# Local heads by pairs, and a new order for two engines around them

## The reference

```python
def window_attention(q, k, v, sink):
    ...
    s = jnp.einsum('bnqhgd,bnkhd->bnhgqk', qb, kb).astype(jnp.float32) / math.sqrt(HEAD_DIM)
    ...
    valid = (jnp.abs(dist) <= WINDOW) & (k_pos[:, None, :] >= 0) & (k_pos[:, None, :] < S)
    s = jnp.where(valid[None, :, None, None], s, NEG_INF)
    ...
    p = jax.nn.softmax(jnp.concatenate([s, sink_b], axis=-1), axis=-1)[..., :-1]
    o = jnp.einsum('bnhgqk,bnkhd->bnqhgd', p.astype(v.dtype), vb)
    return o.reshape(B, S, A_Q_HEADS * HEAD_DIM)
```

## Time and profile before

| | |
|---|---|
| median of 3 runs | 1089.72 us (1089.44 to 1089.85) |
| profiled execution | 1089.0 us, span 1087.1 us |
| PE busy | 1069.8 us, 98% of the span |
| PEld busy | 865.4 us, 80% |
| DVE busy | 726.7 us, 67% |
| ACT busy | 539.7 us, 50% |
| the chain of work that ended last | PE 89%, DVE 7%, ACT 2% |
| granted TensorE clock | full but for the first microseconds (mean 0.995) |

### The profile page before, as it was taken

One profiled execution on the slowest core, in us unless ns is written; L12 is line 12 of the kernel. 1 busy time (PEld: TensorE's weight loads), 2 busy tenths in 40 slices (PEclk: granted clock), 3 DMA queues, 4 the chain that ended last, 5 costly groups with the idle time before them and its releaser, 6 DMA issues.

```text
span 1087.1 us, 14671 instructions
## 1 busy us (share of the span) xinstructions
PE 1069.8 (98%) x4952; PEld 865.4 (80%) x4952; DVE 726.7 (67%) x1224; ACT 539.7 (50%) x829; POOL 37.1 (3%) x40
## 2 busy tenths in 40 slices
PE   8899999999999999999999999999999999999998
PEld 7677678888888778788888888887777888888886
DVE  5756875455557997754555578988868877454553
ACT  6454554444445546644444465547457546444452
POOL 3112000000000210000000000000000000000000
PEclk9899999999999999999999999999999999999999
DMA  9454255565665544455655553544444365655653
GB/s 287 120 167 148 79 167 182 192 190 178 191 193 172 163 152 133 153 180 192 190 178 191 194 172 114 160 155 136 136 138 152 129 199 177 191 182 188 192 184 107
DMA packets 133599, 182.18 MB, mean 168 GB/s; under 512 B 11446, under 2 KB 80322, under 8 KB 133490
## 3 DMA queue, kind: packets, MB, share of 16 engines
q1 hardware_dynamic: 132090, 178.32, 51.7%
q0 software_dynamic: 1056, 2.70, 1.2%
q10 hardware_dynamic: 408, 0.56, 0.1%
HBM read 180.49 MB, written 1.05 MB: 167 GB/s over the span
## 4 chain that ended last, share of the span: by engine, by line
PE 89%; DVE 7%; ACT 2%; issue 1%; DMA 1%; POOL 0%; SPq 0%; DVEq 0%; POOLq 0%; ACTq 0%
PE ps L1844 17%; PE ps L1855 16%; PE ps L1847 16%; PE ps L1865 7%; PE ps L1866 7%; PE ps L1870 7%; PE ps L1829 2%; PE ps L1831 2%; PE ps L1830 2%; DVE wlo L1013 2%; PE ps L1939 1%; PE ps L1922 1%; ACT whi L538 1%; PE ps L2402 1%; PE ps L2069 1%
## 5 line engine op out<-in xcount | busy, mean ns | idle before, releaser
L1013 DVE TENSOR_TENSOR wlo<-raw,whi 128x1024 fp32r<-128x1024 f32 (+1 forms) x338 | 403.7, 1225 | 106.3 <-ACT whi L538 105.3
L538 ACT ACTIVATE whi<-raw 128x1024 fp32r<-128x1024 f32 (+1 forms) x338 | 342.2, 1053 | 102.6 <-DMA raw<-in_ffn_w_out 28.2
L1844 PE MATMUL ps<-whi,ath 128*128 128x512 f32 (+1 forms) x896 | 357.9, 400 | 3.1 <-ACT whi L538 1.4
L1847 PE MATMUL ps<-whi,atl 128*128 128x512 f32 (+1 forms) x896 | 349.7, 391 | 0.0
L1855 PE MATMUL ps<-wlo,ath 128*128 128x512 f32 (+1 forms) x896 | 240.6, 390 | 0.0
L1844 PEld LDWEIGHTS ps<-whi,ath 128*128 128x128 f32 x896 | 168.9, 189 | 47.1 <-issue 8.3
L1855 PEld LDWEIGHTS ps<-wlo,ath 128*128 128x128 f32 x896 | 167.7, 188 | 35.4 <-DVE wlo L1013 0.5
L1847 PEld LDWEIGHTS ps<-whi,atl 128*128 128x128 f32 x896 | 169.1, 189 | 33.0 <-issue 0.5
L1865 PE MATMUL ps<-whi,brh 128*128 128x512 f32 x272 | 106.5, 392 | 0.4 <-issue 0.4
L1866 PE MATMUL ps<-whi,brl 128*128 128x512 f32 x272 | 105.9, 389 | 0.0
L1089 DVE TENSOR_TENSOR brl<-ps,brh 128x512 fp32r<-128x512 f32 x33 | 22.8, 692 | 93.7 <-ACT brh L584 93.7
(11 more groups left out here) (344 smaller groups left out, 1009.1 us busy)
## 6 DMA issues: line engine op xcount, KB each, us to landing
raw<-in_ffn_w_in SPq DMA_DIRECT2D x176, 256.0 KB, 2.9
raw<-in_ffn_w SPq DMA_DIRECT2D x132, 256.0 KB, 2.9
raw<-in_w_in SPq DMA_DIRECT2D x104, 256.0 KB, 2.9
raw<-in_ffn_w_out SPq DMA_DIRECT2D x88, 256.0 KB, 2.8
raw<-in_a_w_in SPq DMA_DIRECT2D x48, 256.0 KB, 4.1
raw<-in_b_w_in SPq DMA_DIRECT2D x48, 256.0 KB, 3.0
raw<-in_a_w_out SPq DMA_DIRECT2D x16, 256.0 KB, 2.9
raw<-in_b_w_out SPq DMA_DIRECT2D x16, 256.0 KB, 2.8
```

Source lines behind the costliest of these rows:

```text
L538: a_(unit_view(whi, slot, w), unit_view(raw, slot, w), ACT.Copy).then_inc(hi_ready, 1)
L1013: v_.tensor_tensor(unit_view(wlo, slot, w), unit_view(raw, slot, w), unit_view(whi, slot, w), ALU.subtract).then_inc(lo_ready, 1)
L1844: mm(ps[bk + t][:, 0:w], ath[:, k, t * P:(t + 1) * P], rh[:, kk, :], start=k == 0, stop=False)
L1847: mm(ps[bk + t][:, 0:w], atl[:, k, t * P:(t + 1) * P], rh[:, kk, :], start=False, stop=False)
```

## The change

Scores and products with the values are issued for two heads at once. `w_scores(i)` takes heads 2i and 2i + 1, alternating between partitions 0 to 63 and 64 to 127 with each matmul; `w_pv(i)` does the same with the two halves of the output. The semaphores count accordingly. `C_L` and the small columns beside it are used in four copies in place of two, so that logits may run up to four heads ahead. `C_PT` still has two, so ACT's copy of a head's transposes now waits for the product pair before. PE's list becomes: between any two pieces of two units one head's transposes; with those of the even heads the score pair for two heads ahead and the product pair before; for the last head the pieces are of one unit. DVE's and ACT's lists are written anew: DVE does the three Newton steps in one go and puts the split of unit `U_C + 47` behind the last `w_out`. No instruction of the three engines is added or left out, but for the semaphores' waits.

```diff
             def w_exp(h):
-                c = sm[:, 128 + 16 * (h % 2):]
+                c = sm[:, 128 + 16 * (h % 4):]
...
             def w_pt(h):
                 act.wait_ge(sem("w_p_turned"), h + 1)
+                if h >= 2:
+                    act.wait_ge(sem("w_pv"), h // 2)
                 a_(C_PT[:, h % 2, :], ps[6 + h % 2][:, :], ACT.Copy).then_inc(sem("w_pt"), 1)
 
             def w_out(i):
-                act.wait_ge(sem("w_pv"), 2 * i + 2)
+                act.wait_ge(sem("w_pv"), i + 1)
                 a_(brh[:, i, :], ps[2 + i % 2][:, 0:S], ACT.Copy).then_inc(sem("w_out_hi"), 1)
...
-            for i in range(WQ + 2):
-                if i == 1:
-                    evac(19, lambda t: C_pd[:, t, 1024:1536], n=4, tiles=(0, 1))
-                if i == 3:
-                    gate_evac(20, 0)
-                if i == 5:
-                    gate_evac(21, 1)
-                if i == 7:
-                    gate_evac(22, 0)
+            w_exp(0)
+            feed(W_STEPS[0])
+            evac(19, lambda t: C_pd[:, t, 1024:1536], n=4, tiles=(0, 1))
+            w_exp(1)
+            w_pt(0)
+            act.wait_ge(sem("h_z"), 4)
+            a_(obh[:, :, :], h_v, ACT.Copy).then_inc(sem("h_hi"), 1)
+            for i in range(WQ // 2):
+
+                feed(W_STEPS[2 * i + 1])
+                if i < 3:
+                    w_exp(2 * i + 2)
                 if i == 0:
-                    w_exp(0)
-                if i < WQ:
-                    feed(W_STEPS[i])
-                if 0 < i < WQ:
-                    w_exp(i)
-                if i == 0:
-                    act.wait_ge(sem("h_z"), 4)
-                    a_(obh[:, :, :], h_v, ACT.Copy).then_inc(sem("h_hi"), 1)
-                if 0 <= i - 1 < WQ:
-                    w_pt(i - 1)
-                if i == WQ:
-                    feed(W_STEPS[WQ])
-                if i == 1:
                     act.wait_ge(evac_act, ACT_EVACS[18])
                     c_squares([(C_z, C_pd[:, 0, 0:1024]), (hid_flat, C_pd[:, 1, 0:512]),
                                (sil_flat, C_pd[:, 1, 512:1024])])
-                if i >= 3 and i % 2 == 1:
-                    w_out((i - 3) // 2)
+                w_pt(2 * i + 1)
+                if i < 3:
+                    feed(W_STEPS[2 * i + 2])
+                    w_exp(2 * i + 3)
+                    gate_evac(20 + i, (0, 1, 0)[i])
+                    w_out(i)
+                    w_pt(2 * i + 2)
+            feed(W_STEPS[WQ])
+            w_out(3)
...
             def w_logits(h):
                 dve.wait_ge(sem("w_scores"), h + 1)
-                if h >= 2:
-                    dve.wait_ge(sem("w_p_turned"), h - 1)
-                c = sm[:, 128 + 16 * (h % 2):]
+                if h >= 4:
+                    dve.wait_ge(sem("w_p_turned"), h - 3)
...
-            for i in range(WQ + 2):
-                if 1 <= i - 1 < WQ:
-                    w_prob(i - 1)
-                if i < WQ:
-                    w_logits(i)
-                if i == 0:
-                    feed(U_C + 32)
-                    w_prob(0)
-
-                if i == 5:
-                    d_sines(0)
-                if i == 6:
-                    d_cosines(0)
-                if i == 7:
-                    d_add(0)
-                    d_sines(1)
-                if i == 8:
-                    d_cosines(1)
-                    d_add(1)
-                    d_scale_keys()
-                if i < WQ:
-                    feed(W_STEPS[i])
-                if i >= 3 and i % 2 == 1:
-                    w_out((i - 3) // 2)
-
-                if i == 1:
-                    dve.wait_ge(sem("h_hi"), 1)
-                    v_.tensor_tensor(obl[:, :, :], h_v, obh[:, :, :], ALU.subtract).then_inc(sem("h_lo"), 1)
-                if i == 2:
-                    c_sums(3, C_z, 320, 16)
-                if i == 3:
-                    c_sums(4, hid_flat, 336, 8)
-                    c_sums(5, sil_flat, 344, 8)
-                if i == 4:
-                    dve.wait_ge(sem("c_ssq"), 6)
-                    link(v_.tensor_scalar(rq_a[:, 0:32], sm[:, 320:352], 1.0 / HD, EPS, ALU.mult, ALU.add))
-                    rsqrt_guess(sm[:, 320:352], 32)
-                if 4 <= i < 7:
-                    rsqrt_step(sm[:, 320:352], 32)
-                if i == 6:
-                    q_scale = sm[:, 320:352].rearrange("p (t h) -> p t h", t=NT)[:, :, 0:8]
-                    link(v_.tensor_scalar(q_scale, q_scale, float(HD) ** -0.5, None, ALU.mult))
+            w_logits(0)
+            feed(U_C + 32)
+            w_prob(0)
+            w_logits(1)
+            feed(W_STEPS[0])
+            w_prob(1)
+            w_logits(2)
+            feed(W_STEPS[1])
+            w_logits(3)
+            dve.wait_ge(sem("h_hi"), 1)
+            v_.tensor_tensor(obl[:, :, :], h_v, obh[:, :, :], ALU.subtract).then_inc(sem("h_lo"), 1)
+            w_prob(2)
+            feed(W_STEPS[2])
+            c_sums(3, C_z, 320, 16)
+            w_prob(3)
+            w_logits(4)
+            feed(W_STEPS[3])
+            w_out(0)
+            w_logits(5)
+            c_sums(4, hid_flat, 336, 8)
+            c_sums(5, sil_flat, 344, 8)
+            w_prob(4)
+            feed(W_STEPS[4])
+            dve.wait_ge(sem("c_ssq"), 6)
+            link(v_.tensor_scalar(rq_a[:, 0:32], sm[:, 320:352], 1.0 / HD, EPS, ALU.mult, ALU.add))
+            rsqrt(sm[:, 320:352], 32)
+            w_prob(5)
+            w_logits(6)
+            feed(W_STEPS[5])
+            w_out(1)
+            w_logits(7)
+            d_sines(0)
+            w_prob(6)
+            feed(W_STEPS[6])
+            q_scale = sm[:, 320:352].rearrange("p (t h) -> p t h", t=NT)[:, :, 0:8]
+            link(v_.tensor_scalar(q_scale, q_scale, float(HD) ** -0.5, None, ALU.mult))
+            w_prob(7)
+            d_cosines(0)
+            d_add(0)
+            feed(W_STEPS[7] - 1)
+            w_out(2)
+            d_sines(1)
+            d_cosines(1)
+            d_add(1)
+            d_scale_keys()
+            w_out(3)
+            feed(W_STEPS[7])
             feed(U_OA + 4)
...
-            def w_scores(h):
-                if h == 0:
+            def w_scores(i):
+
+                if i == 0:
                     pe.wait_ge(sem("c_w_copied"), 3)
-                if h >= 2:
-                    pe.wait_ge(sem("w_l"), 2 * (h - 1))
-                g, pr = h // 4, h // 2
-                rows = slice(64 * (h % 2), 64 * (h % 2) + 64)
+                else:
+                    pe.wait_ge(sem("w_l"), 4 * i)
                 for t in range(NT):
-                    ins = mm(ps[4 + h % 2][:, t * S:(t + 1) * S], C_qT[rows, pr, t * P:(t + 1) * P], C_kT[rows, g, :],
-                             start=True, stop=True)
-                ins.then_inc(sem("w_scores"), 1)
+                    for f in range(2):
+                        rows = slice(64 * f, 64 * f + 64)
+                        ins = mm(ps[4 + f][:, t * S:(t + 1) * S], C_qT[rows, i, t * P:(t + 1) * P],
+                                 C_kT[rows, i // 2, :], start=True, stop=True)
+                ins.then_inc(sem("w_scores"), 2)
...
-            def w_pv(h):
-                pe.wait_ge(sem("w_pt"), h + 1)
-                i = h // 2
-                if h % 2 == 0 and i >= 2:
+            def w_pv(i):
+
+                pe.wait_ge(sem("w_pt"), 2 * i + 2)
+                if i >= 2:
                     pe.wait_ge(sem("w_out_lo"), i - 1)
-                if h == 0:
+                if i == 0:
                     pe.wait_ge(evac_act, ACT_EVACS[18])
-                rows = slice(64 * (h % 2), 64 * (h % 2) + 64)
-                g = h // 4
+                g = i // 2
                 for s in range(2):
-                    ins = mm(ps[2 + i % 2][rows, 0:S], C_pa[:, s, 640 + g * HD:640 + (g + 1) * HD],
-                             C_PT[:, h % 2, s * S:(s + 1) * S], start=(s == 0), stop=(s == 1))
+                    for f in range(2):
+                        rows = slice(64 * f, 64 * f + 64)
+                        ins = mm(ps[2 + i % 2][rows, 0:S], C_pa[:, s, 640 + g * HD:640 + (g + 1) * HD],
+                                 C_PT[:, f, s * S:(s + 1) * S], start=(s == 0), stop=(s == 1))
                 ins.then_inc(sem("w_pv"), 1)
 
+            def w_turn(h):
+                p_turn(h, "w_p", "w_pt", "w_p_turned", C_L[:, h % 4, :])
+
             w_scores(0)
+            units(19, 2, 4)
+            w_turn(0)
             w_scores(1)
-            w_pieces = [(19, 2, 4), (20, 0, 2), (20, 2, 4), (21, 0, 2), (21, 2, 4), (22, 0, 2), (22, 2, 4), (23, 0, 2)]
-            for h in range(WQ + 1):
-                if h < WQ:
-                    units(*w_pieces[h])
-                    p_turn(h, "w_p", "w_pt", "w_p_turned", C_L[:, h % 2, :])
-                if h + 2 < WQ:
-                    w_scores(h + 2)
-                if h >= 1:
-                    w_pv(h - 1)
+            units(20, 0, 2)
+            w_turn(1)
```

(29 more changed lines are left out.)

## The result

The changed kernel took 1078.42 us (median of 4 executions, 1074.50 to 1081.68), the kernel before 1089.58 (4 executions, 1087.35 to 1089.85; three of them are those that the prediction started from): ratio 0.9908, interval 0.988 to 0.9936. The profiled execution, however, took 1081.68 us with a span of 1079.8, and 1079.8 is the span that the prediction gave.

The account below looks back on a forecast made before the run. PE was taken to bound the local heads' 67.17 us; its interludes were to fall from 19.64 to 12.37 us, so 7.3 off the median 1089.72 gave 1082.4 us, range 1081.5 to 1086.3.

Parts of the forecast that it names:

- What bounds the stretch: Eight local heads, 67.17 us: PE sets the length, so PE time spared is won until DVE, idle 8.05, becomes later.
- Score pair 1.07, product pair 1.03: PE, local heads: two heads' scores take 1.07 us and two heads' products 1.03, the array halves running side by side.
- The new interludes, 12.37: PE's local-head work between weight units: 12.37 us in sum against 19.64 before, 7.3 less.
- the reserve of 0.3: PE's unit restarts after half-array work: nine become six, 0.3 us less, left out of the sum against slower pairs.
- DVE's end at 792.0, PE's at 792.6, cover 0.6: End of the stretch: DVE finishes w_out(3) 0.6 us before PE reaches d_turn, the plan's tightest place.
- ACT, the copies and evacuations: ACT in the stretch: the added wait before transpose copies and the gate-block evacuations cost nothing; evac(19) earlier removes a 0.15 wait.
- Behind the stretch: After d_turn: the moved split hides in DVE's 6.01 us of idle time, and later stages move up as a whole.
- Less 7.3: span 1079.8, median 1082.4: Whole kernel: the 7.3 us saved is taken off both the profiled execution's span and the median of 1089.72.
- column halves in turn: Rival for product pairs: scores gain, products don't, 3.4 us dearer, 1085.8; chance 0.12.
- No effect: Rival: all pair records stand 0.216 apart, 1089.3, or each product record waits for its own load, 1089.6; chance 0.03.
- Slower by alternation: Rival for the pairs on PE: alternating heads empties the array at each change of half, 3.7 us more, 1093.4; chance 0.05.
- DVE as the bound: Rival at d_turn: PE waits there for DVE's w_out_lo, 2.3 us given back, 1084.7; chance 0.04.

Follow-up runs that it names:

- p_dve_late: after_port with two extra 128 x 1024 additions on DVE ahead of the last w_out: 1075.39 us.
- p_one_half: after_port with both heads' products of a pair written to partitions 0 to 63, so on one column half: 1076.99 us.
- p_one_row: after_port with both heads of a score pair reading partitions 0 to 63, so on one row half: 1077.34 us.
- before_port: Kernel before the change, with GpSimd's two early additions held until DVE's gate logits are done: 1081.59 us, on another chip 1081.08.
- p_blocked: after_port with each pair issuing both matmuls of one head, then both of the other, instead of alternating: 1073.73 us.
- before_fill: Kernel before the change, with nine useless fp32 matmuls on PE ahead of its wait before turn_qk(0, 0): 1084.77 us.
- after_fill: Changed kernel with the same nine useless matmuls on PE as before_fill: 1077.20 us.
- after_port: Changed kernel with GpSimd's two early additions held until DVE's gate logits are done: 1073.50 us, on another chip 1073.56.

## Why the prediction was right in its terms and wrong in its number

- **What bounds the stretch:** right. PE was busy throughout before and after, and what it was spared was won. p_dve_late shows the limit of that.
- **Score pair 1.07, product pair 1.03:** right; 1.06 and 1.02. That of the products was taken from a single overlap, between bounds of 1.03 and 1.87, so that it came out is partly luck. p_one_half and p_one_row measured both "no overlap" figures, 1.87 and 1.93, as they had been worked out from starts 0.216 apart.
- **The new interludes, 12.37:** measured 1.06 + 1.59 + 4 x 0.36 + 2 x 2.61 + 1.54 + 1.02 = 11.87. The working had put 0.32 of restarts and the 0.09 of the change of layout into them, which in the trace lie outside. The layout change is there: the last product pair starts at 788.52, where four steps of 0.2275 after 787.52 make 788.43. What lies outside, 59.52 - 46.4 - 11.87 = 1.25, is ten restarts of 0.12 on average, the change of layout among them. Interludes and restarts together went from 20.77 to 13.12, 7.65 less: the 7.3 and the reserve of 0.3 that the prediction had set aside.
- **DVE's end at 792.0, PE's at 792.6, cover 0.6:** 791.54, 792.43 and 0.89. The place was right and a little less tight. Its waits for other engines in the stretch are down to these, from 6.1 us to 2.8; most of the 2.2 lies just at the start of the stretch (DVE's split at 732.82):

```profile
DVE wlo L1012 <- ACT whi L538: 2.6, 2, 2.2
...
DVE sm L1628 <- ACT sm L889: 0.2, 1, 0.2
```

- **ACT, the copies and evacuations:** right. PE has no idle time in the stretch, and the second interlude took 1.59 where 1.60 was said.
- **Behind the stretch:** right, 287.37 us against 287.24.
- **The step that failed is the last:** "Less 7.3: span 1079.8, median 1082.4", with a low end of 1081.5. The span is right to the tenth. The step onto the median took it that every execution has the fall of clock of the profiled one, and put the differences between executions at nothing. The three executions of before that it had seemed to say so: they lay within 0.41 us, and that was chance. The range's low end was made from the terms of the sum alone (the reserve, and pairs that start sooner), 0.9 us. What the runs showed in its place: 17 of 36 executions of before and 5 of 12 of the changed kernel have less of the fall or none, and the stop with its fall is worth 6 to 7 us (before at 1082.64 with a mean of 1.000, at 1087.55 to 1089.31 with 0.995; 1081.08 to 1081.59 in before_port). The median of the twelve executions of the changed kernel is 1080.4. The starting value was high too: 1089.72 lies above all 36 later executions of before, on three chips. From the 1088.65 of those with the full fall, less 7.3, the forecast would have been 1081.35, also below the range. The page gave a hint (the mean clock 0.995, an 8 in the second slice of its clock line), but it was read as the first microseconds, and the prediction used the clock of the stretch only.
- **The rivals:** column halves in turn, refuted by the 1.02 against 1.87 of p_one_half. No effect, in either way: refuted by the same rows; by the page of the Trainium skill named in the prediction ("TensorE: Matmul & The Clock Gate", "Part 3: Packing small matmuls") a product pair would have paid its loads, and it took 1.02 us, so the trace disagrees with that rule here. Slower by alternation: refuted by p_blocked. DVE as the bound: didn't come, but was only 0.9 us away.

**Open.** Why the clock falls in some executions and not, or for a shorter time, in others is not shown: every trace of either kernel as given has the fall, since each was of an execution at 0.995. The traces do show that GpSimd's additions start when a DMA lands (31.64 us, released by the filters), so that which of DVE's instructions they catch depends on that moment: L1115 and L1116 in the kernel before, and in the second trace of the changed kernel the first two of the same three (its lines are numbered one less), not the last two:

```profile
31.41 2.50 DVE L1113 SCALAR_TENSOR_TENSOR work<-work 64x256 f32<-64x256 f32 x1
33.95 2.48 DVE L1114 SCALAR_TENSOR_TENSOR work<-work 64x256 f32<-64x256 f32 x1
36.47 0.42 DVE L1115 SCALAR_TENSOR_TENSOR work<-work 64x256 f32<-64x256 f32 x1
```

A later landing alone doesn't shorten the stop. In before_fill the additions start at 33.88 us and catch none of the three (0.42 us each). They catch the three weight splits that DVE does before the gates' logits instead, here below those of the kernel before:

```profile
38.55 3.50 DVE L1013 TENSOR_TENSOR wlo<-raw,whi 128x1024 fp32r<-128x1024 f32 x3 [1.43 <-ACT whi L538]
...
33.72 7.84 DVE L1013 TENSOR_TENSOR wlo<-raw,whi 128x1024 fp32r<-128x1024 f32 x3 [1.43 <-ACT whi L538]
...
33.88 6.60 POOL L483 TENSOR_TENSOR work<-work 64x1024 f32<-64x1024 f32 x2 [7.64 <-DMA work<-in_filt_w]
```

The logits come at 41.49 us, against 41.96 in the kernel before. In after_fill the additions start at 33.51, in the 1.43 us in which DVE waits for ACT before its splits. There the splits take 6.74, about 1 us less. It fits this that the executions with a shorter stop, or none, are those in which the additions fall on idle time of DVE. That is argued, not shown.

## What to carry to other kernels

Small products that fill half of the array were worth pairing on PE here, whether the half is of rows (64 partitions read) or of columns (64 written): the second head came for 0.01 us, and the order within the pair made no difference. Work out from starts what one alone and what two in turn would take; here that gave both ends to 0.01 us. Before moving a sum from a profiled execution to a median, look where the granted clock leaves 1.00 and what made PE stand still there: here one wait, caused by GpSimd far from the change, was worth 6 to 7 us and nearly all of the spread, almost as much as the change itself.

## What was not expected of the hardware

- An addition on GpSimd (64 x 1024, fp32, 2.44 us) held a DVE instruction of 0.42 us for 2.60. In after_port it held an instruction with one tensor input as well (L1112, 1.92 against 0.29), and in before_fill three splits of 3.50 us together for 7.84, while the two additions themselves took 6.60 in place of 4.88.
- In a stop of PE of 4.05 us the granted clock fell to 0.50. It stayed there for 10.24 us, 8.3 of them after work had come back (40.49 + 10.24 - 42.47). Nine useless products of 0.45 us each (4.05 us in all) kept it at 1.00 and made the kernel before 3.3 us faster.
- Two products on different column halves, which read the same 128 partitions, ran fully side by side in fp32, weight loads of 0.136 us included: eight records in 1.02 us, against 1.01 for four.
